# Modulation units moved into the recurrence stages, and token rows of experts 2 to 15 scattered to slot order in DRAM instead of gathered by one-hot products

## What is computed

```python
def modulation(silu_cond, w_mod_l, b_mod_l):            # 1024 -> 6 x 1024, per layer
    m = silu_cond @ w_mod_l + b_mod_l
    return jnp.split(m[:, None, :], 6, axis=-1)

def run_layer(x, silu_cond, lw, rope, ctx):
    sh1, sc1, g1, sh2, sc2, g2 = modulation(silu_cond, lw['w_mod'], lw['b_mod'])
    out, ctx_tensors = token_mixer(modulate(x, lw['norm1'], sh1, sc1), lw, rope, ctx)
    x = x + g1 * out
    x = x + g2 * moe_ffn(modulate(x, lw['norm2'], sh2, sc2), lw)
    return x, ctx_tensors
```

## Time and profile before

| | |
|---|---|
| median of 3 runs | 1552.79 us (1549.07 to 1555.05) |
| profiled execution | 1551.65 us, its span 1549.8 us |
| PE busy | 1383.5 us, 89% of the span |
| DVE, ACT, POOL busy | 534.9 (35%), 335.1 (22%), 241.2 (16%) us |
| bytes moved by DMA | 351.59 MB, mean 227 GB/s |

### The profile page before, as it was taken

One profiled execution on the slowest core, in us unless ns is written; L12 is line 12 of the kernel. 1 busy time (PEld: TensorE's weight loads), 2 busy tenths in 40 slices (PEclk: granted clock), 3 DMA queues, 4 the chain that ended last, 5 costly groups with the idle time before them and its releaser, 6 DMA issues.

```text
span 1549.8 us, 18654 instructions
## 1 busy us (share of the span) xinstructions
PE 1383.5 (89%) x7243; PEld 759.0 (49%) x7244; DVE 534.9 (35%) x1044; ACT 335.1 (22%) x495; POOL 241.2 (16%) x217
## 2 busy tenths in 40 slices
PE   5899999879999899998956999988999788999992
PEld 1455546627545444444523655466654444444541
DVE  1424415735124311212135344278413532112124
ACT  2026524641001101000101065166100100010110
POOL 2530006721001000000012600187100000000001
PEclk9999999999999799999986999999999889999996
DMA  9676441196235999966964331221412644799993
GB/s 347 216 249 221 166 163 55 55 361 228 104 109 206 425 417 429 426 267 249 428 244 142 112 109 55 92 72 55 149 55 109 244 170 183 323 427 426 429 423 136
DMA packets 91412, 351.59 MB, mean 227 GB/s; under 512 B 5880, under 2 KB 13128, under 8 KB 74976
## 3 DMA queue, kind: packets, MB, share of 16 engines
q1 hardware_dynamic: 75840, 317.62, 52.1%
q0 software_dynamic: 6480, 22.41, 4.1%
q10 hardware_dynamic: 9040, 10.84, 2.1%
HBM read 335.30 MB, written 15.55 MB: 226 GB/s over the span
## 4 chain that ended last, share of the span: by engine, by line
PE 80%; DVE 10%; DMA 4%; ACT 3%; issue 2%; POOL 1%; DVEq 0%; SPq 0%; ACTq 0%; POOLq 0%
PE pG L1436 21%; PE pS L1520 15%; PE pG L1428 10%; PE pG L1535 7%; PE pG L1528 6%; PE pG L1666 5%; PE pX L1356 2%; PE pX L1520 2%; DVE ring L1028 2%; PE pG L1389 2%; DMA ring<-in_w_mod_dram 2%; DVE modb L1030 1%; PE pX L1486 1%; DVE gen L1199 1%; PE pS L1462 1%
## 5 line engine op out<-in xcount | busy, mean ns | idle before, releaser
L1436 PE MATMUL pG<-hT,ring 128*128 128x384 f32 x896 | 299.4, 488 | 1.6 <-ACT gen L854 1.6
L1520 PE MATMUL pS<-ring,gen 128*64 128x256 f32 x2048 | 230.4, 383 | 2.2 <-DVE gen L1298 1.9
L1436 PEld LDWEIGHTS pG<-hT,ring 128*128 128x128 f32 x896 | 167.9, 190 | 115.5 <-issue 4.7
L1520 PEld LDWEIGHTS pS<-ring,gen 128*64 128x64 f32 x2048 | 150.1, 138 | 89.7 <-issue 21.8
L1428 PE MATMUL pG<-ring,hT 128*128 128x512 f32 (+1 forms) x384 | 150.3, 549 | 1.4 <-DVE hT L964 0.7
L1305 DVE TENSOR_TENSOR gen<-pS,gen 128x256 f32<-128x256 f32 x32 | 19.7, 617 | 304.6 <-PE pS L1520 304.6
L1535 PE MATMUL pG<-ring,gen 128*64 128x512 f32 x512 | 116.9, 598 | 5.1 <-DVE gen L1311 5.1
L1428 PEld LDWEIGHTS pG<-ring,hT 128*128 128x128 f32 x384 | 72.7, 192 | 72.3 <-issue 67.9
L666 POOL DMA_INDIRECT gen<-y_scr,idx x12 | 12.0, 1003 | 610.1 <-ACTq L904 607.1
L1528 PE MATMUL pG<-hrow,gen 128*64 128x512 f32 x408 | 98.2, 618 | 3.4 <-ACT gen L703 1.9
L883 ACT COPY gen<-pG 128x512 f32<-128x512 f32 x32 | 18.8, 586 | 336.7 <-PE pG L1535 336.7
(11 more groups left out here) (278 smaller groups left out, 1629.4 us busy)
## 6 DMA issues: line engine op xcount, KB each, us to landing
ring<-in_w_exp_up_dram SPq DMA_DIRECT2D x32, 2048.0 KB, 16.4
ring<-in_w_exp_down_dram SPq DMA_DIRECT2D x32, 2048.0 KB, 14.0
ring<-in_w_exp_gate_dram SPq DMA_DIRECT2D x32, 2048.0 KB, 13.8
ring<-in_w_mod_dram SPq DMA_DIRECT2D x24, 2048.0 KB, 9.2
ring<-in_w_in_dram SPq DMA_DIRECT2D x20, 2048.0 KB, 8.5
modb<-mod_scr POOLq DMA_DIRECT2D x20, 512.0 KB, 11.2
y_scr<-gen ACTq DMA_DIRECT2D x72, 128.0 KB, 7.7
ring<-in_w_out_dram SPq DMA_DIRECT2D x4, 2048.0 KB, 10.5
```

The lines of the kernel that those rows point to most:

```text
L1436: ins = pe.matmul(ps[:, 0:TOK], w[:, k, c0:c0 + P], src[:, k, :], start=(k == 0), stop=(k == nk - 1))
L1520: ins = pe.matmul(dst[64 * hf:64 * hf + 64, 0:256], x[:, k, :], w[:, k, 256 * hf:256 * (hf + 1)], start=(k == 0), stop=(k == KC - 1))
```

## The change

**1. Modulation units.** Of the units behind hq, ff, fb and i only two pairs stay (4, 5 behind hq and 6, 7 behind fb). Units 8 to 15 go into layer 0's level stage and 16 to 23 into layer 1's, one per step: TensorE does ga j, `mod_sum` of the unit before, lev j, `mod` of this unit; ScalarE does the sigmoid, `mod_store` of the unit before, the exps, `mod_copy`. After the last step `mod_sum` and `mod_store` of the last unit stand ahead of wba and of the final exps. Nothing of it is left behind the recurrence or in the router. A load takes the slot whose last reader comes first, instead of slots in turn.

**2. Token rows.** `gather64` is gone. Experts 0 and 1 get xT directly from one product (`gather01`: 24 products of 128 columns, copied out by ScalarE in two halves). For the others POOL scatters the three tiles of `hrow` twice (a token has two experts) by index into a DRAM buffer `x_scr` in slot order, waits until all six have landed, and loads 64 rows per expert back into `xrow` (two buffers, 128 KB twice per expert). A further block's rows come from `x_scr` too; the first is loaded by POOL, the next by ScalarE. `x_scr` (1856 rows of 4 KB, 7.6 MB) is set to zero once, by 15 SP DMAs after the load of the last wo unit in layer 0. The wait on `route_ready` moves from ahead of the first expert to behind its down part on TensorE. Two transposes of the next rows stand ahead of the activations' transposes and two behind.

```diff
-MOD_BEHIND = {"hq": 4, "ff": 6, "fb": 8, "i": 10}
-MOD_LEV = 12
-MOD_LATE = 20
+MOD_BEHIND = {"hq": 4, "fb": 6}
+MOD_LEV = 8
...
+    for j in range(KC):
+        m = MOD_LEV * (L + 1) + j
+        gs += [("ga", j)] + [("ms", m - 1)] * (j > 0) + [("mod", m)]
...
+                    if (L, name) == (0, ("wo", 1)):
+                        for r in range(0, XROWS - BLK, P):
+                            sp.dma_start(x_scr[r:r + P, :].rearrange("p (a c) -> p a c", a=4),
+                                         bc(zeros, [P, 4, 256], 1)).then_inc(x_zero, 16)
...
+                pool.wait_ge(x_zero, X0)
+                pool.wait_ge(route_ready, L + 1)
+                for t in range(NT):
+                    for c in range(2):
+                        pool.indirect_dma_start(x_scr[:, :], bass.IndirectOffsetOnAxis(ap=idx[:, c, t:t + 1], axis=0),
+                                                hrow[:, t, :], None).then_inc(x_put, 16)
+                pool.wait_ge(x_put, 16 * 2 * NT * (L + 1))
...
+                def load_rows(row, dst, s):
+                    for hf in range(2):
+                        pool.dma_start(dst[BLK * hf:BLK * (hf + 1), :],
+                                       x_scr[bass.ds(row, BLK), 512 * hf:512 * (hf + 1)]).then_inc(s, 16)
+
+                for j in range(2):
+                    load_rows((2 + j) * BLK, xrow[j], x_got[j])
+                load_rows(NE * BLK, xrow_o, xo_first)
+                with pool.Fori(1, NLOAD // 2) as p:
+                    for j in range(2):
+                        pool.wait_ge(e_xTp, p * 2 + (NLOAD * L + j - 1))
+                        load_rows(p * (2 * BLK) + (2 + j) * BLK, xrow[j], x_got[j])
...
                     act.activation(mergedT[:, j, :], ps[:, 0:TOK], ACT.Sigmoid).then_inc(ga_ready, 1)
+                    m = MOD_LEV * (L + 1) + j
+                    if j > 0:
+                        mod_store(L, m - 1)
                     lev(L, j + 1)
+                    mod_copy(L, m)
+                mod_store(L, m)
...
                     cols(L, ("ga", j), w, P * (j % 4), hT, KC)
+                    m = MOD_LEV * (L + 1) + j
+                    if j > 0:
+                        mod_sum(L, m - 1)
                     lev(L, j)
-                if L == 0:
-                    for m in range(MOD_LEV, MOD_LATE, 2):
-                        mod(m)
-                        mod(m + 1)
-                        mod_sum(m)
-                        mod_sum(m + 1)
+                    mod(L, m)
+                mod_sum(L, m)
...
-                        pe.wait_ge(e_P, p * 2 + (L * NPOS + j + 2))
-                        pe.wait_ge(e_xrow, m + 1)
-                        gather64(bank[0], Pm).then_inc(e_gather, 1)
-                        pe.wait_ge(e_act, n + 2)
-                        turn(bank[5], actb, 2).then_inc(e_aTp, 1)
-                        pe.wait_ge(e_xrow, m + 2)
-                        turn(bank[4], xrow, 4).then_inc(e_xTp, 1)
...
+                    if turned:
+                        pe.wait_ge(x_got[1 - j], p * 32 + (NLOAD // 2 * 32 * L + 32 * j))
+                        turn(bank[4], xrow[1 - j], 2)
+                    pe.wait_ge(e_act, n + 2)
+                    turn(bank[5], actb, 2).then_inc(e_aTp, 1)
+                    if turned:
+                        turn(bank[4], xrow[1 - j], 4, 2).then_inc(e_xTp, 1)
```

More of the change, by code:

```diff
@@ L41, with mix_units @@
 YROWS = (NE + MAX_EXTRA) * BLK
+XROWS = YROWS + BLK
 FAR = 10000.0
-NGATH = NE + 1
-NPOS = NE + 2
+NLOAD = NE - 2
 MODS = 12
 MOD_FIRST = 4
-MOD_BEHIND = {"hq": 4, "ff": 6, "fb": 8, "i": 10}
-MOD_LEV = 12
-MOD_LATE = 20
[L53 to L59, removed]
+MOD_BEHIND = {"hq": 4, "fb": 6}
+MOD_LEV = 8
+def mix_units(L):
+    lev = [("mod", MOD_LEV * (L + 1) + j) for j in range(KC)]
+    units = [("mod", m) for m in range(MOD_FIRST)] if L == 0 else []
+    for kind in ("q", "kv", "hq", "ff", "fb", "i", "g"):
+        units.append((kind, 0))
+        if L == 0 and kind in MOD_BEHIND:
+            units += [("mod", MOD_BEHIND[kind] + i) for i in range(2)]
+    return (units + [("ga", 0)] + lev[:4] + [("ga", 1)] + lev[4:]
+            + [("wba", 0), ("gh", 0), ("gh", 1), ("wbh", 0), ("wo", 0), ("wo", 1)])
+MIX_UNITS = [mix_units(L) for L in range(DEPTH)]
 MIX_SLOTS = 4
@@ L89, in mod_groups, with groups, unit_slots, held_before @@
     return [(kind, m + i) for m in range(first, last, 2) for kind in ("mod", "ms") for i in range(2)]
[L92 to L100, removed]
+def groups(L):
+    gs = [("mod", m) for m in range(MOD_FIRST)] if L == 0 else []
+    for kind in ("q", "kv", "hq", "ff", "fb", "i", "g"):
+        gs += [(kind, i) for i in range(HH if kind in ("hq", "ff", "fb") else NT)]
+        if L == 0 and kind in MOD_BEHIND:
+            gs += mod_groups(MOD_BEHIND[kind], MOD_BEHIND[kind] + 2)
+    for j in range(KC):
+        m = MOD_LEV * (L + 1) + j
+        gs += [("ga", j)] + [("ms", m - 1)] * (j > 0) + [("mod", m)]
+    return (gs + [("ms", m)] + [("wba", j) for j in range(KC)] + [(k, j) for j in range(KC) for k in ("gh", "wbh")]
+            + [("wo", n) for n in range(2 * NT)])
+GROUPS = [groups(L) for L in range(DEPTH)]
 ALL_GROUPS = [(L, g) for L in range(DEPTH) for g in GROUPS[L]]
 GROUP_NO = {lg: n for n, lg in enumerate(ALL_GROUPS)}
+def unit_slots(L):
+    slots, held = [], []
+    for n, u in enumerate(MIX_UNITS[L]):
+        s = n if n < MIX_SLOTS else held.index(min(held))
+        held[s:s + 1] = [GROUP_NO[L, last_group(u)]]
+        slots.append(s)
+    return slots, held
+UNIT_SLOT = [unit_slots(L)[0] for L in range(DEPTH)]
+SLOT_LOADS = [[UNIT_SLOT[L].count(s) for s in range(6)] for L in range(DEPTH)]
+FIRST_EXPERTS = [sorted(range(MIX_SLOTS), key=lambda s: unit_slots(L)[1][s]) + [4, 5] for L in range(DEPTH)]
+def held_before(L, n):
+    return max(i for i in range(n) if UNIT_SLOT[L][i] == UNIT_SLOT[L][n])
 ATT_STEPS = 4 * NT
```

324 lines of the change are left out of this document (148 added, 176 removed).

## The result

The kernel before takes 1555.31 us (median of 11 runs), the changed kernel 1544.61 (11 runs, 1536.66 to 1549.81). The ratio is 0.9934 with a 95% interval of 0.9913 to 0.9955: faster by 0.7%, or 11 us, where 53 were forecast, and the time lies outside the range (1472 to 1532). The profiled run of the changed kernel took 1544.22 us with a span of 1542.5, so the stages of its trace can be laid beside those of the kernel before.

The account below looks back on a forecast made before the run. In the expert stage TensorE set the pace at 14.74 us per expert, with DMA only 4% behind at 15.4. The terms summed to -53.0 us on the profiled 1551.65, giving 1499 us, range 1472 to 1532.

Parts of the forecast that it names:

- Parts 1 to 4: Layer 0/1: projections -11.8 us (layer 0 only), level stages +12.7 each, recurrence end -25.7/+5, router to first expert -5.4/+1.2.
- Part 5: Zeroing by 15 SP DMAs in gh/wo, 18 us of DMA: costs nothing.
- Part 6: Expert stages: PE 12.4 us an expert, DMA becomes the bound at 16.1; -28.3 us in layer 0, -13.4 in layer 1.
- B: DMA-bound experts: row loads cost DMA time out of proportion or slow the weights; slower than before, 1574 at 3.8 us; chance 0.08.
- E: Expert stage does not change at all, DMA having bound it already: +42, 1541 us; chance 0.05.
- A: Level stage hides nothing, 27.5 us instead of 12.7 in each layer: 1529 us; chance 0.11.
- C: Rows late at the start or a unit's weights late, 5 to 15 us: 1510; chance within the forecast's 0.65.
- D: Experts: period stays near 15.4 us and the clock holds at the first expert: 1478 us; chance 0.11.

Follow-up runs that it names:

- e1: Kernel before with only the modulation units moved, experts still gathering by one-hot products; 1541.52 us, ratio 0.9916.
- e3: Changed kernel without the row loads of experts 4 to 15, which compute on the rows of experts 2 and 3; 1501.36 us, ratio 0.9647.
- e6: Changed kernel with every row load of experts 2 to 15 done twice, the second copy into spare space; 1576.23 us, ratio 1.0124.
- e11: Changed kernel with half rows on partition 2s+h: an expert's rows come in one DMA over all 128 partitions, 2 KB pieces in order; 1515.02 us, ratio 0.9737.
- e13: Changed kernel with an expert's rows in two DMAs, left halves to even and right halves to odd partitions; 1512.67 us, ratio 0.9729.
- e4: Changed kernel with the row loads of experts 4 to 15 issued by ScalarE's hardware queue instead of POOL; 1536.58 us, ratio 0.9889.
- e8: Changed kernel with row loads of experts 4 to 15 as one DMA of 32 partitions x 8 KB into spare space; 1540.23 us, ratio 0.9904.
- e14: Changed kernel with row source in order, as two DMAs of 32 rows, to partitions 0 to 63 and 64 to 127; 1544.81 us, ratio 0.9925.
- e5: Changed kernel with an expert's rows in one 256 KB DMA over all partitions, its pattern beginning with an axis of two; 1569.66 us, ratio 1.0090.
- e15: Changed kernel with both row DMAs of experts 4 to 15 sent to partitions 32 to 95 of spare space; 1519.85 us, ratio 0.9780.
- e2: Kernel before with only the token rows going through DRAM, modulation units left where they were; 1571.26 us, ratio 1.0103.

## Why the prediction was wrong

**What bounds the kernel.** Right. The two limits 4% apart were there: a PE-bound expert fell to 12.5 us, PE waits for `ring<-in_w_exp` from the fifth expert on in layer 0 (I had said about the seventh), and the DMA is the bound.

**Parts 1 to 4, modulation and router.** Right in size. A pair of level steps takes 264.02 - 241.46 = 22.6 us (23.6 forecast, 20.0 in the earlier trace rows), and the level stages grew by 11.3 and 13.0 us (12.7 forecast each). The path through them was not the one described: every step now takes 11.28 us and PE waits nowhere in layer 0's stage, so the 1.7 us that ScalarE's part was to add in each even step does not show, and all of PE's waits were filled. Further, layer 0's wait for wba of the earlier trace rows is gone. First projection to gh: -23.2 and +16.7 for -24.8 and +17.7. End of wo to the first gate: -5.9 and +2.6 for -5.4 and +1.2. e1 shows the sum by itself.

**Part 5, zeroing.** As forecast: from gh to the end of wo, where it stands, layer 0 takes 105.8 us in both kernels.

**Part 6, the step that failed.** The row loads were costed at 0.62 us by their bytes and 0.69 by the store queue, "which moves the same size". The stores of the earlier trace rows are of the same size and also on half the partitions, but they go from SBUF to DRAM. The loads go the other way, the way of the weight stream, and cost 17.1 - 15.4 = 1.7 us in layer 1 (1.8 by e3, 1.6 by e6). The mechanism of the sum, DMA as the bound and a period set by bytes, was right: in the form of e11 the period is 16.0 us, forecast 16.1, and e13's stages of experts are 254.1 and 261.3 us against the forecast 244.7 and 259.6 and the changed kernel's 269.9 and 275.7. So of the 41 us by which these stages came out longer than forecast (40 as a difference to the kernel before, for which the sum took 273.0 in both layers), 30 are the partitions.

**The rest of part 6.** Of the other 11 us layer 0 has 9. The forecast let its loads go on 3.5 us after the first gate. In the trace SP's next load leaves at 503.18, 5.8 us after the gate at 497.38 (6.7 us in e13), which is 2 to 3 of the 9. The scatter had the DMA nearly to itself, as forecast: it runs from 493.4 to 504.4, and the last weights before it had landed at 487.8. But the first six row loads, for experts 2 and 3 and the further block, leave from 504.6 on, beside the weights. Windows of the changed kernel, then of e13:

```profile
512.00:516.00 4.00, 4.00 (x42) 2.63 (x39) 0.00 (x0) 0.38 (x1) 0.00 (x0) 1.00 1.00 322
516.00:520.00 4.00, 3.37 (x22) 1.50 (x20) 1.62 (x3) 0.00 (x0) 1.05 (x2) 1.00 0.96 324
520.00:524.00 4.00, 2.09 (x10) 0.57 (x7) 0.00 (x0) 0.59 (x1) 0.00 (x0) 1.00 1.03 345
```

```profile
500.00:504.00 4.00, 3.33 (x32) 1.93 (x28) 0.57 (x1) 0.38 (x1) 0.64 (x2) 1.00 0.71 253
...
512.00:516.00 4.00, 3.97 (x36) 2.33 (x32) 0.35 (x1) 0.38 (x1) 0.00 (x0) 1.00 0.99 411
516.00:520.00 4.00, 3.39 (x18) 1.44 (x20) 1.28 (x3) 0.00 (x0) 1.11 (x2) 1.00 1.02 348
520.00:524.00 4.00, 4.00 (x38) 2.33 (x36) 0.00 (x0) 0.58 (x1) 0.00 (x0) 1.00 1.04 420
```

Part of the loss at 512 to 524 is the half-partition loads again; what is left in e13, a reserve of weights that starts smaller, is argued from these windows and was not tried by itself. The `issue` row at 522.09 of the chain above, 2.8 us ahead of the third expert's gate, is a wait for which the profile names nothing; e13 does not have it, and its cause is open.

**The rivals.** B named the right mechanism (row loads that cost DMA time out of proportion, or lower the rate of the weights) and the right place. But it was weighed only as far as it makes the change a loss, at 2.9 us an expert and more, and not at the degrees between: at p = 17.1 to 17.5 it gives 1499 + 24 x 1.0 to 1.4 = 1523 to 1533, most of the way to the 1544.6. I had given it 0.08 and let the range end at 1532. Its reason was wrong, though: small pieces and POOL's queue were not it (e4, e8), and the 3.8 us estimated from the Trainium skill (DMA: Bandwidth & Descriptors, Measured (HBM→SBUF, 128 partitions, SWDGE, issued from GpSimd)) is over twice what was measured. E, whose 1541 is nearly the result, was right by number alone, and by luck: the DMA had not bound the stages before; they gained on PE and lost about as much on the DMA. A, C and D did not come about, but for 2 us in layer 1 where expert 2's rows come late.

What would have pointed to it beforehand stood unused: the row loads cover half the partitions each, as the diff says, and the Trainium skill (SBUF — State Buffer, Door 1) says which ports such a load reaches. The store queue was the nearest row and still the wrong direction. An unknown cost whose only row goes the other way needed an upper end well above 0.7 us.

## What to carry to other kernels

Where weights stream at the DMA's limit, a small load beside them is paid by the partitions it lands on: here 1.7 us for 0.26 MB in two DMAs that each lie on one side of partition 64, 0.6 us in DMAs that each lie on both sides. Lay such tiles out so that each DMA covers both sides (every second partition, or all of them in one DMA) and undo it in a copy that is made anyway; keep the larger axis outermost in the pattern. Price a transfer from a row of the same direction, and when a change removes work from the engine that leads by 4%, put the care into the price on the other resource.

## What the runs showed of the hardware that was not expected

- Two loads into SBUF, one on partitions 0 to 63 and one on 64 to 127, pull the whole rate from 425 to about 380 GB/s while they are in flight (383 in the window shown above, 259 in the lowest of e14's 1.5 us slices), at a DMA share that stays at 1.0. The 345 and 340 GB/s in the expectations of e5 and e15 are too low for the mean. By the rate that the Trainium skill (the same section on Door 1) gives for one side, about 218 GB/s, an estimate of their cost is 0.26 MB / 218 = 1.2 us; measured 1.7. Stores from half the partitions showed nothing of it: the rate is 425 GB/s in e11, with them and with its row loads.
- The same 256 KB over all partitions took 8.0 us to land as 2 KB pieces in order (e11) and 30.7 us in a pattern that begins with an axis of two (e5), in packets of 512 bytes.
- The last of six scatters took 39.9 us to land beside a refilling ring (e2); with the ring full it was issued at 499.8 and had landed when the row loads left at 504.6 (changed kernel).
